# One layer of a Conformer, RWKV-7 and mixture-of-experts trunk: an earlier slot for small transposes, another order of loads, the last expert not split, the last store in two halves

## The chip, the cores and the metric

The kernel runs on one core of a Trainium2 chip. TensorE (PE) multiplies matrices; VectorE (DVE), ScalarE (ACT) and GpSimd (POOL) do the rest of the arithmetic, and SyncE (SP) issues most DMAs, in the order of its own program. Each engine runs its instructions in order and waits at semaphores. The metric is the time of one execution on the device, in microseconds (us), as the median of several runs; lower is better.

## The reference, cut to what matters

All data is float32. There are 520 tokens (512 of one prompt, 8 samples of one token each), a model width of 1024 and one layer.

```python
z = x @ w_in                                   # 2720 columns
u = z_a * sigmoid(z_gate)                      # group A: 512 channels
c = silu(layer_norm(causal_depthwise_conv(u, width=31)))
zs = z_rw + (z_prev - z_rw) * mu_shift         # group B: 8 heads of 64
r, k, v, wd, ad, gd = split(zs)
decay = exp(-exp(-softplus(-(w0 + tanh(wd) @ w_up)) - 0.5)); a = sigmoid(a0 + ad @ a_up)
S = S * decay + (S a_t) b_t^T + v_t k_t^T;  y_t = S r_t     # per token and head
x = layer_norm(ALPHA * x + concat(c, o_rw) @ w_out)
scores = sigmoid(x @ router_w)                 # 64 experts, 8 per token, group-limited
moe = shared_expert(x) + sum_e gate_e * ((silu(x @ G_e) * (x @ U_e)) @ D_e)
y = layer_norm(ALPHA * x + moe)
```

The kernel also returns the last conv inputs, the last shifted row and the recurrence state, for prompt and samples.

## The kernel before

The program has two blocks, with a meeting of all engines between them.

**Projection (`prepare`).** x is transposed, and the projection goes by columns of up to 128 outputs: `col(c)` does 8 steps over the contraction, with 2 matmuls of 260 tokens in each, so 16 matmuls; each shows as two records in the trace (float32). The order of the columns is `COLS`: two pairs for the conv gate (columns 0 to 3), the LoRA column (4), then k and r of each group of heads, and so on. `col(c, halfway)` calls `halfway()` after four of the eight steps, so that small work of PE sits inside a column. ACT drains a finished column out of PSUM (`drain`, L341 to L352), DVE shifts it (`shift`, L692 and L694) and, in between, adds up the 31 taps of the conv, one instruction per tap and channel group (`Taps.take`, L161 and L163; 124 in all). The number of taps between two steps is written out by hand.

Two helpers turn small inputs: `turn_small` transposes the conv weights, parameter vectors and shift rows, and waits for all 13 small loads (`small_loaded`), which ACT issues from 12.43 us on, after its copies of the transposed x; `turn_conv_rows` transposes the samples' conv rows (L492). DVE copies both out and does the samples' part of the conv (L659 to L679) before the first `glu` (L684) and the first taps. The loads of columns 4 and later each wait for the column four places before.

**Recurrence, mixing and routing (`recur_and_mix`).** The recurrence goes over 16 chunks of 32 tokens, with 16 steps on PE (L1392) and DVE (L1964 to L1997) in turn, and other work is put between the steps by tables (`CENTRE`, `TURN`, ...). SP's program is a list: waits and DMAs in one order. Of the names: `row_taken` counts PSUM tiles that ACT has drained, `step_done` the steps, `move_done` the chunk products; `w_out_half` are the two halves of w_out, used first by `mix_part` (L1498); `scr_y` is a detour through memory that lays the samples' y out as rows, read by `centre` (L1870) for the last but one tile; `load_up(sp, m, q)` and `load_down(sp, m, q)` fetch 1 MB each of expert q into slot q mod 6; `x_rows` are rows of x, needed for the layer norm after the mix.

**Experts (`experts`).** All 64 experts run in order, each on a list of up to 96 tokens. PE: `make_list` (L869), `gate_up` (L2297) for the next expert, `turn_list` (L2272) for the one after, `down` (L2325) for this one. ACT and DVE turn gate and up into the hidden values (`gate_act` L2306, `gate_mul` L2313 and L2315) and weigh the result (L2335 on ACT, L2343 on DVE). POOL adds the weighted rows to the tokens in memory with an indirect DMA (`add_rows`, L2352); each such scatter waits until the one before has landed:

```python
        pool.wait_ge(y_act, q + 1)
        pool.wait_ge(y_dve, q + 1)
        if job.has_before(1):
            pool.wait_ge(added[(s + 1) % 2], 16 * job.before)
```

For the last pair of experts the order is special: PE does the gate half of expert 63, then `down` of 62, then the up half of 63, then `down` of 63. After the last scatter SP reads the token rows back in five tiles, ACT and DVE normalise them (`shift_row`, L2261, is the last step of a tile), and SP stores them (L2388).

## Time and profile before

| | us |
|---|---|
| median of 3 runs | 1150.96 |
| all three runs | 1150.25, 1150.96, 1155.59 |
| profiled execution, time | 1150.96 |
| profiled execution, span from first to last instruction | 1148.6 |
| PE busy | 1081.4 |
| DVE busy | 537.3 |
| ACT busy | 280.1 |
| POOL busy | 180.3 |

The profile is of one execution. A row of the timeline gives start, duration, engine, line of the kernel, operation, the tensors written and read, shape, count, and in brackets how long the engine had been idle and who released it. PEld is PE's weight load, which runs beside its matmuls. PEclk is the clock that PE was granted: 1.00 is 2.4 GHz, 0.50 is 1.2 GHz. SPq and ACTq rows are DMA issues, not transfers.

### The profile page before, as it was taken

The page shows a single profiled execution, that of the slowest core. Times are in us where ns is not written, and L with a number is a line of the kernel's source. Part 1 is how long each engine was busy: PE and PEld are TensorE (multiplying, and loading weights), DVE is VectorE, ACT ScalarE, POOL GpSimd, SP SyncE. Part 2 cuts the span into 40 slices and gives each one's busy share as a digit, 9 for nine tenths or more (in the row PEclk, how much of TensorE's full clock was granted, in tenths as well). Part 3 has the DMA queues.
Part 4 walks back from the last instruction along what each step waited for, and adds up shares of the span by engine and source line. Part 5 has one row for each costly group of instructions (what it writes and reads, how often), then busy time and mean ns, then how long its engine had stood idle before and what let it go on. Part 6 is the DMA issues. An engine that isn't in the chain of part 4 may idle for free.

```text
span 1148.6 us, 33461 instructions
## 1 busy us (share of the span) xinstructions
PE 1081.4 (94%) x14966; PEld 820.4 (71%) x14967; DVE 537.3 (47%) x1204; ACT 280.1 (24%) x596; POOL 180.3 (16%) x198
## 2 busy tenths in 40 slices
PE   8999998888989999999999999999999999999990
PEld 6877886766653467777777777777777777777760
DVE  0888959699565787553222222222222222222215
ACT  2156411132427111111111111111111111111114
POOL 2000100000000002122222222222222122222310
PEclk9999998988679999999999999999999999999996
DMA  7222231320416547799999999999999999999724
GB/s 214 74 56 56 55 82 35 55 68 5 161 39 225 183 162 296 287 358 367 368 363 366 372 359 359 362 361 358 368 369 353 355 368 359 360 360 360 217 37 159
DMA packets 87364, 278.79 MB, mean 243 GB/s; under 512 B 22331, under 2 KB 46916, under 8 KB 62381
## 3 DMA queue, kind: packets, MB, share of 16 engines
q1 hardware_dynamic: 71941, 239.29, 56.9%
q0 software_dynamic: 14336, 34.11, 12.4%
q10 hardware_dynamic: 944, 3.24, 0.8%
q8 instruction: 119, 1.95, 0.7%
q14 instruction: 24, 0.20, 0.0%
HBM read 258.80 MB, written 34.52 MB: 255 GB/s over the span
## 4 chain that ended last, share of the span: by engine, by line
PE 67%; DVE 9%; ACT 2%; issue 2%; DMA 1%; SPq 0%; POOLq 0%; DVEq 0%; ACTq 0%
PE ph L2297 30%; PE ph L2325 19%; PE pst L2272 4%; PE ph L1498 2%; PE pz_late L2272 2%; DVE w_exp L163 2%; PE ph L1453 1%; PE pt L869 1%; PE pst L1392 1%; PE ph L1624 1%; PE ph L1480 1%; PE pz_late L1436 1%; PE pz_late L1437 1%; PE pt L1411 0%; PE pz_late L1521 0%
## 5 line engine op out<-in xcount | busy, mean ns | idle before, releaser
L2297 PE MATMUL ph<-arena,w_exp 128*64 128x96 f32 x8192 | 352.6, 247 | 0.0
L2297 PEld LDWEIGHTS ph<-arena,w_exp 128*64 128x64 f32 x8192 | 340.5, 138 | 4.2 <-issue 3.1
L2325 PE MATMUL ph<-w_exp,arena 128*96 128x512 f32 x512 | 230.5, 593 | 1.5 <-DVE arena L2315 1.5
L2352 POOL DMA_INDIRECT scr_f<-arena,row x64 | 91.9, 1436 | 472.2 <-DVE row L889 265.2
L2313 DVE TENSOR_TENSOR arena<-arena,ph 128x192 f32<-128x192 f32 x64 | 22.7, 354 | 294.3 <-ACT arena L2306 294.3
L507 PE MATMUL pz<-w_exp 128*128 128x260 f32 x672 | 158.8, 394 | 0.3 <-ACT w_exp L322 0.3
L2325 PEld LDWEIGHTS ph<-w_exp,arena 128*96 128x96 f32 x512 | 80.2, 167 | 104.0 <-issue 102.3
L507 PEld LDWEIGHTS pz<-w_exp 128*128 128x128 f32 x672 | 129.6, 196 | 23.7 <-issue 3.1
L2343 DVE TENSOR_SCALAR arena<-ph,weight 96x512 f32<-96x512 f32 x64 | 47.8, 746 | 168.0 <-PE ph L2325 167.9
L2306 ACT ACTIVATE arena<-ph 128x192 f32<-128x192 f32 x64 | 21.1, 330 | 426.1 <-PE ph L2297 419.4
L163 DVE SCALAR_TENSOR_TENSOR w_exp<-arena,w_exp 128x512 f32<-128x512 f32 x120 | 90.0, 750 | 3.8
L900 POOL DMA_INDIRECT x_area<-scr_x,row x64 | 63.4, 990 | 39.6 <-issue 34.1
L2335 ACT ACTIVATE arena<-ph,weight 96x512 f32<-96x512 f32 x64 | 43.7, 682 | 81.4 <-PE ph L2325 81.4
L1498 PE MATMUL ph<-w_exp 128*128 128x512 f32 x128 | 57.0, 597 | 1.2 <-DVE w_exp L2035 1.2
L2272 PE MATMUL pst<-ident,x_area 96*128 96x96 f32 x320 | 50.8, 289 | 0.0
L869 PEld LDWEIGHTS pt<-table,member 128*96 128x96 bf16 x320 | 24.3, 124 | 36.1 <-issue 35.7
L2272 PEld LDWEIGHTS pst<-ident,x_area 96*128 96x128 f32 x320 | 40.3, 202 | 7.7 <-issue 0.4
L1498 PEld LDWEIGHTS ph<-w_exp 128*128 128x128 f32 x128 | 23.6, 190 | 30.1 <-issue 28.4
L2282 ACT COPY arena<-pst 128x480 f32<-128x480 f32 x64 | 35.7, 558 | 35.0 <-PE pst L2272 33.9
L858 DVE TENSOR_TENSOR member<-slot_index,position 128x480 bf16<-128x480 f32 x64 | 41.6, 651 | 0.0
L2272 PE MATMUL pz_late<-ident,x_area 96*128 96x96 f32 x192 | 31.8, 275 | 0.0
L1480 PE MATMUL ph<-x_area,w_exp 128*128 128x260 f32 x128 | 29.1, 385 | 0.7 <-ACT arena L1829 0.7
(358 smaller groups left out, 1083.5 us busy)
## 6 DMA issues: line engine op xcount, KB each, us to landing
w_exp<-in_exp_up_dram SPq DMA_DIRECT2D x64, 1024.0 KB
w_exp<-in_exp_down_dram SPq DMA_DIRECT2D x64, 1024.0 KB
w_exp<-in_exp_gate_dram SPq DMA_DIRECT2D x64, 1024.0 KB
w_exp<-in_w_in_dram SPq DMA_DIRECT2D x22, 512.0 KB, 3.9
w_exp<-in_x_prompt_dram SPq DMA_DIRECT2D x8, 512.0 KB, 5.3
w_exp<-in_w_out_dram SPq DMA_DIRECT2D x2, 2048.0 KB, 11.5
scr_x<-arena SPq DMA_DIRECT2D x4, 512.0 KB
scr_f<-arena ACTq DMA_DIRECT2D x4, 512.0 KB, 4.5
```

The lines of the kernel that those rows point to most:

```text
L163: self.ch.link(self.nc.vector.scalar_tensor_tensor(out, u, w, out, ALU.mult, ALU.add))
L507: last = nc.tensor.matmul(banks(pz[0:w, c % 2, :])[:, b, :], m.w_col[:, c % WB, k, 0:w], halves(m.x_t[:, k, :])[:, b, :], start=(k == 0), ...
L858: nc.vector.tensor_tensor(m.member[:, s % 2], m.slot_index[:].unsqueeze(1).broadcast_to([P, NT, CAP]), src.unsqueeze(2).broadcast_to([P, N ...
L900: nc.gpsimd.indirect_dma_start(m.x_list[:, s, :], None, m.scr_x1, bass.IndirectOffsetOnAxis(ap=m.row[:, job.l:job.l + 1], axis=0), bounds_ ...
L1480: last = nc.tensor.matmul(banks(ph[:, 1 - part, :])[:, b, :], sh_w[part][:, k, j * P:(j + 1) * P], halves(x1_t[:, k, :])[:, b, :], start=( ...
L1498: last = nc.tensor.matmul(ph[0:n, i % 2, c * 512:(c + 1) * 512], lhs, w_out[c][:, kw, :], start=(part == 0 and k == 0), stop=(part == 1 an ...
L2272: last = nc.tensor.transpose(px[bank][:, at * CAP:(at + 1) * CAP], v[:, k, :], m.ident[0:CAP, 0:CAP])
L2297: last = nc.tensor.matmul(pgu[64 * half:64 * half + 64, s % 2, (2 * part + j) * CAP:(2 * part + j + 1) * CAP], w[job.slot][:, k, f0:P * ha ...
L2325: last = nc.tensor.matmul(pyl[0:CAP, c, :], hid[:, s % 2, j, :], m.expert_down[job.slot][:, j, c * 512:(c + 1) * 512], start=(j == 0), sto ...
L2335: nc.scalar.activation(y_list[:, s % 2, 0:512], pyl[0:CAP, 0, :], ACT.Copy, scale=weight[:, job.l:job.l + 1]).then_inc(y_act, 1)
L2343: nc.vector.tensor_scalar(y_list[:, s % 2, 512:1024], pyl[0:CAP, 1, :], weight[:, job.l:job.l + 1], None, ALU.mult).then_inc(y_dve, 1)
L2352: nc.gpsimd.indirect_dma_start(m.scr_f, bass.IndirectOffsetOnAxis(ap=row[:, job.l:job.l + 1], axis=0), y_list[:, s % 2, :], None, bounds_c ...
```

## The change

Four places change. First, `turn_small` moves from the middle of column 1 to behind column 0, and `turn_conv_rows` from the middle of column 2 to the middle of column 1. PE's instructions there, before (each row one kind of instruction with its count; `pz` is the projection's PSUM tile, `pt` the transposes'):

```order
L466 MATMUL pt<-ident,w_exp 128x128 x32
L469 MATMUL pt<-ident,w_exp 128x8 x8
L507 MATMUL pz<-w_exp 128x260 x24
L477 MATMUL pt<-ident,w_exp 128x39 x4
L482 MATMUL pt<-ident,w_exp 128x9 x14
L482 MATMUL pt<-ident,w_exp 32x9
L507 MATMUL pz<-w_exp 128x260 x16
L492 MATMUL pt<-ident,w_exp 128x120 x8
L507 MATMUL pz<-w_exp 128x260 x56
```

and in the changed kernel:

```order
L466 MATMUL pt<-ident,w_exp 128x128 x32
L469 MATMUL pt<-ident,w_exp 128x8 x8
L507 MATMUL pz<-w_exp 128x260 x16
L477 MATMUL pt<-ident,w_exp 128x39 x4
L482 MATMUL pt<-ident,w_exp 128x9 x14
L482 MATMUL pt<-ident,w_exp 32x9
L507 MATMUL pz<-w_exp 128x260 x8
L492 MATMUL pt<-ident,w_exp 128x120 x8
L507 MATMUL pz<-w_exp 128x260 x72
```

Sixteen matmuls are column 0, 24 are one and a half columns. The transposes of L477 and L482 are `turn_small`, those of L492 `turn_conv_rows`; eight matmuls moved from ahead of the first to behind it, and sixteen from ahead of the second to behind.

Second, SP's list in the second block has the loads of w_out ahead of the samples' detour through `scr_y`, drops the wait for the last step ahead of the x rows, and has two expert loads ahead of the waits for the layer-norm rows. Before:

```order
L1193 DMA scr_y<-arena 128x32
L1195 DMA x_area<-scr_y 8x512
L1198 DMA w_exp<-in_w_out_dram 128x8x512 x2
L1200 DMA arena<-in_router_w_dram 128x8x64
L1201 DMA arena<-in_router_bias_dram 128x64
L1205 DMA w_exp<-in_x_prompt_dram 128x1024 x2
L1208 DMA w_exp<-in_ln_g_dram 128x1024
L1209 DMA w_exp<-in_ln_b_dram 128x1024
L1210 DMA w_exp<-in_sh_up_dram 128x8x256
L1211 DMA w_exp<-in_sh_down_dram 128x2x1024
L919 DMA w_exp<-in_exp_up_dram 128x2048
L925 DMA w_exp<-in_exp_down_dram 128x2048 x2
```

and changed:

```order
L1195 DMA w_exp<-in_w_out_dram 128x8x512 x2
L1197 DMA scr_y<-arena 128x32
L1199 DMA x_area<-scr_y 8x512
L1201 DMA arena<-in_router_w_dram 128x8x64
L1202 DMA arena<-in_router_bias_dram 128x64
L1205 DMA w_exp<-in_x_prompt_dram 128x1024 x2
L920 DMA w_exp<-in_exp_up_dram 128x2048
L926 DMA w_exp<-in_exp_down_dram 128x2048
L1210 DMA w_exp<-in_ln_g_dram 128x1024
L1211 DMA w_exp<-in_ln_b_dram 128x1024
L1212 DMA w_exp<-in_sh_up_dram 128x8x256
L1213 DMA w_exp<-in_sh_down_dram 128x2x1024
```

The two `w_out` loads moved up by two rows, and expert 1's up and expert 0's down from the end of this piece to behind the x rows (expert 3's down follows it).

Third, the last pair of experts has the common order. The end of PE's expert work (L2297 is gate and up, 64 matmuls; L2325 is down, 4), before:

```order
L2297 MATMUL ph<-arena,w_exp 64x96 x64
L2272 MATMUL pst<-ident,x_area 128x96 x5
L2272 MATMUL pz_late<-ident,x_area 128x96 x3
L2325 MATMUL ph<-w_exp,arena 96x512 x4
L2297 MATMUL ph<-arena,w_exp 64x96 x32
L2325 MATMUL ph<-w_exp,arena 96x512 x4
L2297 MATMUL ph<-arena,w_exp 64x96 x32
L2325 MATMUL ph<-w_exp,arena 96x512 x4
```

and changed:

```order
L2298 MATMUL ph<-arena,w_exp 64x96 x64
L2274 MATMUL pst<-ident,x_area 128x96 x5
L2274 MATMUL pz_late<-ident,x_area 128x96 x3
L2325 MATMUL ph<-w_exp,arena 96x512 x4
L2298 MATMUL ph<-arena,w_exp 64x96 x64
L2325 MATMUL ph<-w_exp,arena 96x512 x8
```

The second half (up) of expert 63 moved ahead of `down` of 62. ACT and DVE follow: `gate_act` and `gate_mul` of 63 stand ahead of the weighing of 62.

Fourth, the last tile's last DVE step and its store are split into two halves of 512 columns.

```diff
@@ projection, PE
                 col(0)
-                col(1, turn_small)
-                col(2, turn_conv_rows)
+                turn_small()
+                col(1, turn_conv_rows)
+                col(2)
@@ second block, SP
+                sp.wait_ge(row_taken, use["col", 2 * LATE - 1] + 1)
+                for c in range(2):
+                    sp.dma_start(m.w_out_half[c][:], ...).then_inc(m.w_out_loaded[c], 16)
                 sp.wait_ge(sample_y_ready, 1)
                 sp.dma_start(m.scr_y..., s_y[:]).then_inc(sample_y_stored, 16)
                 sp.wait_ge(sample_y_stored, 16)
                 sp.dma_start(sample_y, m.scr_y).then_inc(sample_y_loaded, 16)
-                sp.wait_ge(row_taken, use["col", 2 * LATE - 1] + 1)
-                for c in range(2):
-                    sp.dma_start(m.w_out_half[c][:], ...).then_inc(m.w_out_loaded[c], 16)
...
                 sp.wait_ge(move_done, 2 * TM)
-                sp.wait_ge(step_done, NCH)
                 for i in range(2):
                     sp.dma_start(x_rows[:, i, :], ...).then_inc(x_loaded[i], 16)
+                load_up(sp, m, 1)
+                load_down(sp, m, 0)
                 sp.wait_ge(y_done, TM)
                 sp.wait_ge(state_ready, NCH + 1)
...
-                load_up(sp, m, 1)
-                load_down(sp, m, 0)
                 load_down(sp, m, 3)
@@ shift_row(dve, at, i, parts=1)
+        for c in range(parts):
+            cs = slice(D // parts * c, D // parts * (c + 1))
+            nc.vector.scalar_tensor_tensor(f_scaled[i][0:n, cs], ...).then_inc(out_ready, 1)
@@ experts, SP: the last store
+        for c in range(2):
+            sp.wait_ge(out_ready, NT + c)
+            cs = slice(D // 2 * c, D // 2 * (c + 1))
+            sp.dma_start(m.y_prompt[T - P:T, cs], f_scaled[TM - 1][:, cs]).then_inc(out_stored, 16)
@@ experts, PE
-                gate_up(pe, Job(q + 1), (0, 1) if q + 2 < E else (0,))
+                gate_up(pe, Job(q + 1))
...
             down(pe, Job(q))
-            if q + 2 == E:
-                gate_up(pe, Job(q + 1), (1,))
@@ experts, DVE (ACT alike)
-            if q + 2 < E:
+            if q + 1 < E:
                 gate_mul(dve, Job(q + 1))
...
             weigh_dve(dve, Job(q))
-            if q + 2 == E:
-                gate_mul(dve, Job(q + 1))
@@ the last tile
-        shift_row(dve, TM, TM - 1)
+        shift_row(dve, TM, TM - 1, 2)
```

## Rows read from the trace of the kernel before

**Rows 1.** Page, part 1: engine, busy us (share of the span), instructions.
```profile
PE 1081.4 (94%) x14966; PEld 820.4 (71%) x14967; DVE 537.3 (47%) x1204; ACT 280.1 (24%) x596; POOL 180.3 (16%) x198
```

**Rows 2.** Windows: stretch, length, busy us by engine, PEclk, DMA share, GB/s.
```profile
300.00:360.00 60.00, 53.02 (x783) 32.09 (x772) 34.20 (x60) 28.67 (x79) 0.00 (x0) 0.80 0.54 182
560.00:700.00 140.00, 140.00 (x2084) 108.77 (x2083) 36.53 (x126) 25.70 (x55) 33.78 (x28) 1.00 1.02 365
```

**Rows 3.** Timeline, PE at the start: start us, us, what, [idle before <-releaser].
```profile
12.69 10.79 PE L507 MATMUL pz<-w_exp 128*128 128x260 f32 x48 [0.30 <-ACT w_exp L322]
23.65 0.44 PE L477 MATMUL pt<-ident,w_exp 39*128 39x39 f32 x4 [0.18 <-DMA w_exp<-in_state_conv_dram]
25.00 7.28 PE L507 MATMUL pz<-w_exp 128*128 128x260 f32 x32
```

**Rows 4.** Timeline, all engines, the same columns, 32 to 70 us.
```profile
32.73 1.22 DVE L665 COPY w_exp<-pt 128x480 f32<-128x480 f32 x2 [7.20 <-PE pt L492]
37.90 0.70 DVE L684 TENSOR_TENSOR arena<-arena 128x520 f32<-128x520 f32 x1
51.28 0.71 ACT L352 ACTIVATE w_exp<-pz,w_exp 128x520 f32<-128x520 f32 x1
56.48 0.75 DVE L692 SCALAR_TENSOR_TENSOR w_exp<-arena,w_exp 128x512 f32<-128x512 f32 x1
58.13 1.11 PE L514 MATMUL pa<-w_exp,arena 64*128 64x260 f32 x4 [0.47 <-ACT w_exp L413]
69.11 0.75 DVE L692 SCALAR_TENSOR_TENSOR w_exp<-arena,w_exp 128x512 f32<-128x512 f32 x1 [2.99 <-ACT w_exp L352]
```

**Rows 5.** Windows of 1 us, PE alone: length, busy, PEclk, DMA.
```profile
257.00:258.00 1.00, 0.00 (x0) 1.00 0.00 0
258.00:259.00 1.00, 0.00 (x0) 1.00 0.00 0
260.00:261.00 1.00, 1.00 (x14) 0.50 0.07 16
263.00:264.00 1.00, 1.00 (x5) 0.92 0.00 0
```

**Rows 6.** Timeline of SP; then page, part 6: issues, KB, us to landing.
```profile
297.41 0.35 SPq L1193 DMA_DIRECT2D scr_y<-arena  x1
300.94 1.03 SPq L1198 DMA_DIRECT2D w_exp<-in_w_out_dram  x2
w_exp<-in_w_out_dram SPq DMA_DIRECT2D x2, 2048.0 KB, 11.5
```

**Rows 7.** Chain of waits in order of time: start us, us, what.
```profile
327.70 0.57 DVE arena L1870
343.63 3.63 PE ph L1498 x8
```

**Rows 8.** Timeline, all engines, the last expert.
```profile
1113.91 2.86 PE L2297 MATMUL ph<-arena,w_exp 128*64 128x96 f32 x64
1115.61 1.40 POOL L2352 DMA_INDIRECT scr_f<-arena,row  x1 [4.99 <-DVE arena L2343]
1118.22 3.67 PE L2325 MATMUL ph<-w_exp,arena 128*96 128x512 f32 x8 [1.45 <-DVE arena L2315]
1121.94 0.75 DVE L2343 TENSOR_SCALAR arena<-ph,weight 96x512 f32<-96x512 f32 x1 [3.77 <-PE ph L2325]
1123.53 1.40 POOL L2352 DMA_INDIRECT scr_f<-arena,row  x1 [6.52 <-DVE arena L2343]
```

**Rows 9.** Chain of waits, the last scatter.
```profile
1123.53 4.73 DMA scr_f<-arena,row
```

**Rows 10.** The scatter tensor scr_f: DMA time from issue to landing.
```profile
DMA to landing us min/median/max: 3.7/8.6/10.3
```

**Rows 11.** Timeline, the last row of the output.
```profile
1144.30 1.28 DVE L2261 SCALAR_TENSOR_TENSOR w_exp<-w_exp,arena 128x1024 f32<-128x1024 f32 x1
```

**Rows 12.** Windows of 1 us, DVE alone, DMA share and GB/s last.
```profile
1145.00:1146.00 1.00, 0.58 (x1) 0.50 0.97 389
```

More of the change, by code:

```diff
@@ L1191, in _ @@
                         sp.dma_start(m.new_shift_s[:, c0:c0 + w], tail_rows[1:1 + B, t % 2, 0:w]).then_inc(tails_stored[t % 2], 16)
+                sp.wait_ge(row_taken, use["col", 2 * LATE - 1] + 1)
+                for c in range(2):
+                    sp.dma_start(m.w_out_half[c][:], m.w_out[:, c * 512:(c + 1) * 512].rearrange("(k p) n -> p k n", p=P)).then_inc(m.w_out_loaded[c], 16)
                 sp.wait_ge(sample_y_ready, 1)
@@ L1195, in _ @@
                 sp.dma_start(sample_y, m.scr_y).then_inc(sample_y_loaded, 16)
-                sp.wait_ge(row_taken, use["col", 2 * LATE - 1] + 1)
-                for c in range(2):
-                    sp.dma_start(m.w_out_half[c][:], m.w_out[:, c * 512:(c + 1) * 512].rearrange("(k p) n -> p k n", p=P)).then_inc(m.w_out_loaded[c], 16)
                 sp.wait_ge(w2_done, TM)
@@ L2255, in invert_root, with shift_row @@
         nc.vector.reciprocal(aggr[0:n, i, 3:4], aggr[0:n, i, 2:3]).then_inc(inverted, 1)
-    def shift_row(dve, at, i):
+    def shift_row(dve, at, i, parts=1):
         n = TOK_TILES[i][1]
@@ L2260, in shift_row @@
         dve.wait_ge(scaled, at + 1)
-        nc.vector.scalar_tensor_tensor(f_scaled[i][0:n, :], f_scaled[i][0:n, :], aggr[0:n, i, 3:4], ln2_b[0:n, :],
-                                       ALU.mult, ALU.add).then_inc(out_ready, 1)
+        for c in range(parts):
+            cs = slice(D // parts * c, D // parts * (c + 1))
+            nc.vector.scalar_tensor_tensor(f_scaled[i][0:n, cs], f_scaled[i][0:n, cs], aggr[0:n, i, 3:4], ln2_b[0:n, cs],
+                                           ALU.mult, ALU.add).then_inc(out_ready, 1)
     def turn_list(pe, job):
@@ L2283, in copy_turned, with gate_up @@
                            px[bank][:, 0:(k1 - k0) * CAP].rearrange("p (k t) -> p k t", t=CAP)).then_inc(x_ready, 1)
-    def gate_up(pe, job, parts=(0, 1)):
+    def gate_up(pe, job):
         q, s = job.q, job.s
@@ L2289, in gate_up @@
             pe.wait_ge(hid_ready, q - 1)
-        for part in parts:
-            w = (m.expert_gate, m.expert_up)[part]
+        for part, w in enumerate((m.expert_gate, m.expert_up)):
             pe.wait_ge((m.gate_loaded, m.up_loaded)[part][job.slot], job.filled)
@@ L2299, in gate_up @@
                                                 start=(k == 0), stop=(k == KD - 1))
-        if 1 in parts:
-            last.then_inc(gu_done, 1)
+        last.then_inc(gu_done, 1)
     def gate_act(act, job):
@@ L2383, in sync @@
             sp.dma_start(f[i][0:n, :], m.scr_f[t0:t0 + n, :]).then_inc(f_loaded[i], 16)
-        for at, i in enumerate(ORDER):
+        for at, i in enumerate(ORDER[:-1]):
             t0, n = TOK_TILES[i]
@@ L2388, in sync @@
             sp.dma_start(dst, f_scaled[i][0:n, :]).then_inc(out_stored, 16)
-        sp.wait_ge(out_stored, 16 * NT)
+        for c in range(2):
+            sp.wait_ge(out_ready, NT + c)
+            cs = slice(D // 2 * c, D // 2 * (c + 1))
+            sp.dma_start(m.y_prompt[T - P:T, cs], f_scaled[TM - 1][:, cs]).then_inc(out_stored, 16)
+        sp.wait_ge(out_stored, 16 * (NT + 1))
     def tensor(pe):
@@ L2527, in scalar @@
         for q in range(E):
+            if q + 1 < E:
+                gate_act(act, Job(q + 1))
             if q + 2 < E:
-                gate_act(act, Job(q + 1))
                 copy_turned(act, Job(q + 2))
             weigh_act(act, Job(q))
-            if q + 2 == E:
-                gate_act(act, Job(q + 1))
         def body(k, ex):
```

## The prediction

> **What bounds the kernel now.** I read the page first. PE is busy for 94% of the span [rows 1]: 67 us of idle time is all that any reordering can touch, unless it takes work away, and this change takes none. Next came the windows by stage. From 560 to 700 us PE is busy for 140.00 of 140 us at full clock [rows 2]; the 64 experts run like that from about 480 to 1100 us, one after the other, with PE never waiting for a weight, though the DMA engines are as full as PE. Nothing in the change touches that stretch, so it only slides in time. What is left are four places where instructions move: the first columns of the projection, SP's queue around the recurrence, the last expert, and the last store. For these I read PE's timeline at both ends, VectorE's (DVE) and ScalarE's (ACT) beside it, SP's issues, and the chain of waits.
>
> In the projection PE and DVE take turns at being last. PE starts its columns at 12.69 us and runs them without a gap of note [rows 3]. DVE sits idle for 7.20 us until the transposes at L492 are there, starts its tap work at 37.90, and then leads for a while: at 58.13 PE waits 0.47 us for a tanh (L413) whose input DVE shifts at 56.48. At 69.11 it has turned round: DVE waits 2.99 us for the drain of column 6, which comes straight behind PE's matmuls [rows 4].
>
> **The small transposes.** Before, they stand in the middle of column 1 and find their data just landed: PE waits 0.18 us at 23.65 for the last of the small loads [rows 3]. The order now puts them behind column 0. Issue of those loads is not changed (ACT issues them after its copies of x), so they still land at 23.6. The work taken from in front of them is half a column: 16 of the 32 records that take 7.28 us [rows 3], 3.64 us. So PE reaches them at about 20.0 and stands for about 3.65 us. Nothing is gained back on PE: the half column is still to be done. Column 1 ends 4.5 us later (its second half, and L492 too, now follow), column 2 and all after it 3.64 later.
>
> DVE gains at first. L492 has 16 matmuls less ahead of it and, with the stall, comes 3.5 us earlier, so its small work and the first taps start that much sooner. It would reach the shift of the LoRA column (L692, 56.48) at 53.0. But the drain of that column ended at 51.28+0.71=51.99 [rows 4] and comes 3.64 later, at 55.6. DVE goes on at 55.6, 0.9 us sooner than before, which takes away PE's 0.47 us at 58.13; PE is then 3.64-0.47=3.17 us late. At 69.11 DVE was already waiting for PE's column, so it is 3.17 late too, and DVE, PE and ACT go through the rest of the projection with the same distances. All engines meet at the end of this part, near 224 us. I take 3.2 us, whole, on the path. Bounds from the rows: 0 if later waits of this kind swallow it, 3.7 if the 0.47 is not won back.
>
> **The clock behind that stall.** The slices from 257 to 259 us hold no work of PE; its granted clock, 1.00 (2.4 GHz) in them, is 0.50 (1.2 GHz) at 260, with PE working again, and 0.92 at 263 [rows 5]. Such a stretch of some 3.3 us at half clock costs 1.7 us when the work in it is dense. The new stall is longer than those two slices, so I expect a fall behind it. Ends: 0 (the clock holds) and 1.7. I take 1.3, as part of the stretch may lie in the stall itself. The Trainium skill (TensorE: Matmul & The Clock Gate, section "HAM oscillation — how this bites in real kernels") says that a wait for a DMA between dense groups of matmuls can bring the clock down each time; by that rule the case with the fall stands, 1155.6 us, and without it the sum would be 1154.3. The rows agree with the rule at 256 us.
>
> **SP's queue.** The load of w_out, 4 MB, goes from 300.94 to where the store of scr_y stood, 297.41 [rows 6]. Its first user is the mix at 343.63 [rows 7], over 40 us later: nothing gained. Behind it now queue on SP the store and reload of the sample rows; they may land as late as w_out does, 11.5 us after its issue [rows 6], with about 3 us more for the way out and back (300.94 less 297.41 is 3.5): about 312 us. Their reader is the centring of the last but one tile (L1870) at 327.70 [rows 7], so 15 us of cover remain, and with both sides shifted by the same 3 to 5 us it stays so. The x rows no longer wait for step 16, and loads of expert 1's up and expert 0's down go ahead of the layer-norm rows; these 3 MB run between 312 and 325 us, when nothing else loads. Behind the wait that remains, the layer-norm rows meet 2 MB less in front of the shared weights. No PE or DVE wait in the profile ends on any of these, so I price it at 0. Bounds: 0.5 us either way, about the 0.47 that a wait cost in [rows 4]; the covers named would have to vanish for more.
>
> **The last expert.** Before: gate of 63, down of 62, up of 63, a wait of 1.45 us for the ACT/DVE steps, down of 63. Now gate and up of 63, down of 62 (under which those steps hide), down of 63. PE ends 1.45 us sooner. But down of 62 ends 2.86 us later (the up part, [rows 8]). POOL's scatter of 62 started at 1115.61 and would start at 1118.5. Each scatter waits for the one before to land; the last took 4.73 us from POOL's start [rows 9]. So 62 lands at 1123.2. The last scatter started at 1123.53, 0.84 us after its DVE step (1121.94+0.75=1122.69). Now its DVE step is ready at 1121.2, but the landing at 1123.2 holds it; with 0.1 to 0.84 us to get going it starts between 1123.3 and 1124.1. I take 1123.7: 0.2 us later than before, so PE's gain is gone. Bounds: -1.45 (all of it comes through) and +0.6. With the shortest landing of the run, 3.7 us [rows 10], it would be -0.9.
>
> **The last store.** The last DVE step took 1.28 us for 1024 columns [rows 11]; 512 cost 0.75 (L692, [rows 4]), so both halves end 0.2 us later, the first 0.5 us sooner. The store of the tile before is still running at 1145 to 1146, 389 GB/s with the engines at 0.97 [rows 12]: the halves queue behind it, and their 512 KB take 1.35 us as before. Only the small gap between two stores can close. I take -0.1; bounds -0.5 and +0.3. The Trainium skill (DMA: Bandwidth & Descriptors, section "Anatomy of one DMA — SWDGE (gpsimd) path") gives a DMA a fixed 2.0 us plus bytes over 436 GB/s; by that an estimate for the half as last store would be 0.6 us less, minus the 0.2 on DVE. That fit is for another kind of queue, and no run here shows it.
>
> **Sum.** 3.2 + 1.3 + 0 + 0.2 - 0.1 = 4.6 us. The profiled execution has a span of 1148.6 us and a time of 1150.96 us, which is also the median of the three runs. 1150.96+4.6 = 1155.6 us, 0.4% slower.
>
> **Rivals.**
> The clock holds (0.14): only the stall remains, 1154.3 us. For it: the stall follows full-clock work, and the wait of 1.45 us at the last expert leaves the clock at 1.00. Against: [rows 5].
> The early start of DVE decides (0.08), the other side: if DVE's tap work and not PE's columns sets the end of the projection, the 3.5 us that DVE gains at 32.73 come through, and with +0.1 at the end the time is 1147.5 us. It decides if the 2.99 us wait at 69.11 goes away. Against: that wait is DVE's, for PE [rows 4]. About a third of this case, with luck elsewhere, would read as faster by over 0.5%.
> The last expert pays (0.08): the scatter of 62 lands fast enough that the 1.45 us come through: 1154.0 us.
> More half clock in the recurrence (0.20): between 300 and 360 us the granted clock is 0.80 on average [rows 2], which is 24 us at half clock, in stretches behind short idle times of PE. All of that is shifted against whatever decides when the clock is looked at. The three runs before lie 5.3 us apart; a further 2 to 3 stretches at 1.7 us each are 4.4 us: 1160 us.
>
> **How the numbers follow.** The main case has 0.50, its own range is 1153.5 to 1158. A measurement of this kernel can tell about 0.5% (5.8 us) from no change, so over 1156.7 us counts as slower. Of the main case I give 0.14 to that side and 0.36 to the same. Slower: 0.14+0.20=0.34. Same: 0.36+0.14+0.05+0.08=0.63. Faster: 0.03. The range runs from 1151.5 to 1160: below it lies most of the DVE case, above it half of the clock case.
>
> **What would show it.** A PE idle of 3.5 to 3.8 us in front of L477 at 23.6, on a DMA; a clock of 0.50 in some slice between 23 and 29; the drains of columns 2 to 5 some 3.6 us later; DVE's small work from 29.3; the LoRA shift waiting for ACT at 55.6; the next part starting 3 to 5 us later. At the end: no wait before the last L2325, and the last scatter waiting for a scatter, not for DVE. It would be wrong if the small loads landed at 20, if the projection ended no later than before, or if the experts, from first to last, took another time than before.

## The result: about 9 us slower, and outside the range

The changed kernel took 1162.8 us (median of 5 runs, 1160.7 to 1163.3) against 1153.0 us for the kernel before beside it: a ratio of 1.0077, 95% interval 1.0049 to 1.0104. Run once more beside its parts (e8 below) it was 1.0082 [1.0066, 1.0099], 9.5 us. The prediction said 1155.6 us, 1151.5 at least and 1160 at most. The base also moved: the kernel before, 1150.96 us in the three runs shown, had medians of 1153.0 to 1155.1 in the comparisons, and its profile is of a quick execution. So ratios are compared here, not times. On the base that the prediction used, the two ratios are 1159.8 and 1160.4 us, the edge of its range; the change itself is twice the 4.6 us that it forecast.

| stretch | before | changed | more |
|---|---|---|---|
| start to block 2 (DVE's first row of it) | 224.1 | 230.7 | 6.6 |
| block 2 to the issue of ln_g | 119.6 | 124.9 | 5.3 |
| from there to the gate of expert 63 | 763.8 | 764.6 | 0.8 |
| gate of 63 to the end of the span | 41.1 | 42.2 | 1.1 |
| span | 1148.6 | 1162.4 | 13.8 |

The profiled pair is further apart than the medians, 13.8 us against 9 to 10, because that execution of before was quick in its first stretch. The page's first part of the changed kernel answers to [rows 1]; PE's busy time is nearly the same, so the loss is idle time:

```profile
PE 1083.0 (93%) x14966; PEld 821.7 (71%) x14967; DVE 537.4 (46%) x1205; ACT 280.8 (24%) x596; POOL 179.9 (15%) x198
```

The windows of the changed kernel, as in [rows 2] (length, busy time by engine, PEclk, DMA share, GB/s). The experts run as before. From 300 to 360 us PE works 5.3 us less (all is shifted, so it is not the same work), at a lower clock:

```profile
300.00:360.00 60.00, 47.75 (x1037) 33.31 (x1032) 32.24 (x59) 21.36 (x60) 0.83 (x4) 0.77 0.43 145
560.00:700.00 140.00, 140.00 (x2059) 107.88 (x2060) 37.13 (x126) 26.00 (x56) 32.15 (x27) 1.00 1.03 359
```

The same work compared, block 2 up to the issue of ln_g (PE alone: length, busy, PEclk, DMA share, GB/s), the kernel before first: PE is busy 0.9 us less and its mean clock is no lower, but it is idle for 22.8 us and not 16.6. So what this stretch lost is idle time, not clock:

```profile
224.09:343.69 119.60, 103.02 (x2944) 0.81 0.22 69
230.66:355.60 124.94, 102.12 (x2944) 0.82 0.25 83
```

PE's timeline at the start, changed kernel, as in [rows 3] (start us, us, what, idle before and releaser):

```profile
12.13 7.28 PE L507 MATMUL pz<-w_exp 128*128 128x260 f32 x32 [0.30 <-ACT w_exp L322]
24.38 0.65 PE L477 MATMUL pt<-ident,w_exp 39*128 39x39 f32 x4 [4.96 <-DMA w_exp<-in_state_conv_dram]
24.96 1.68 PE L482 MATMUL pt<-ident,w_exp 9*128 9x9 f32 x15
26.57 6.57 PE L507 MATMUL pz<-w_exp 128*128 128x260 f32 x16
```

The wait is there, 4.96 us and not 3.65: the columns begin 0.56 us sooner than in [rows 3], and the transposes, which wait for the last load, 0.73 us later. Behind it 16 records of the projection take 6.57 us; in [rows 3] 32 take 7.28, so 16 are 3.64. The clock had already fallen inside the wait, and stayed down. Windows of 1 us show both ends of the stretch:

```profile
23.00:24.00 1.00, 0.00 (x0) 0.00 (x0) 0.00 (x0) 0.00 (x0) 0.00 (x0) 0.50 0.55 167
31.00:32.00 1.00, 1.00 (x4) 0.74 (x3) 0.00 (x0) 0.00 (x0) 0.00 (x0) 0.50 0.00 0
33.00:34.00 1.00, 1.00 (x10) 1.00 (x9) 0.41 (x1) 0.00 (x0) 0.00 (x0) 1.00 0.00 0
```

DVE, as in [rows 4]. The copy of L492 begins at 33.59, 0.86 us later than before, not 3.5 earlier; the slow half column took the gain. The waits for ACT's drains are 2.66 us at the LoRA shift and 4.59 at the shift of column 6, r (2.99 before):

```profile
33.59 1.22 DVE L666 COPY w_exp<-pt 128x480 f32<-128x480 f32 x2 [6.50 <-PE pt L492]
59.97 0.75 DVE L693 SCALAR_TENSOR_TENSOR w_exp<-arena,w_exp 128x512 f32<-128x512 f32 x1 [2.66 <-ACT w_exp L352]
76.48 0.75 DVE L693 SCALAR_TENSOR_TENSOR w_exp<-arena,w_exp 128x512 f32<-128x512 f32 x1 [4.59 <-ACT w_exp L352]
```

SP's timeline, as in [rows 6]: w_out goes at 304.45, the detour's store behind it, and its reload only at 319.18, 13.7 us after the store (3.2 before):

```profile
304.45 1.03 SPq L1195 DMA_DIRECT2D w_exp<-in_w_out_dram  x2
305.52 3.71 SPq L1197 DMA_DIRECT2D scr_y<-arena  x1
319.18 0.30 SPq L1199 DMA_DIRECT2D x_area<-scr_y  x1
```

No engine waits for those sample rows: DVE reads them at 342.82 (L1870). But PE stands, a few us behind the issue of w_out, in the middle of its chunk products (L1376) and of a step (L1392), for "issue", that is for nothing that the profile shows. First the kernel before, then the changed one:

```profile
300.85 0.27 PE L1376 MATMUL ph<-w_exp 32*64 32x64 f32 x2 [0.62 <-issue]
304.84 1.00 PE L1392 MATMUL pst<-x_area,w_exp 64*64 64x64 f32 x13 [1.41 <-issue]
```
```profile
311.70 0.27 PE L1376 MATMUL ph<-w_exp 32*64 32x64 f32 x2 [3.63 <-issue]
318.07 1.01 PE L1392 MATMUL pst<-x_area,w_exp 64*64 64x64 f32 x13 [2.40 <-issue]
```

The same instructions of the program, with 2.03 us of idle time before and 6.03 now. The page's part 3 has a queue for instructions, with the same row in both kernels (packets, MB, share), and one window of 0.5 us, from 309.0, in the changed kernel has one packet of it inside PE's idle time, with the DMA engines full of w_out (third fence, a window of 2 us: DMA share 1.06, 392 GB/s last):

```profile
q8 instruction: 119, 1.95, 0.7%
```
```profile
q8 instruction: 1, 0.02, 13.5%
```
```profile
308.00:310.00 2.00, 0.07 (x3) 0.00 (x0) 1.93 (x5) 1.09 (x5) 0.00 (x0) 1.00 1.06 392
```

119 packets for 1.95 MB are 16 KB each. PE and its weight load have 29,933 instructions in the span, some 250 for each packet, and the packets come as PE's instructions do: 3.3 to 4.2 us apart among the small matmuls of the recurrence, 6 to 10 us apart in the experts. So it looks as if blocks of PE's instructions were fetched while the program runs, by the same DMA engines that move w_out. That became the theory to test. (The Trainium skill, Trainium Architecture — The Big Picture, section "The software stack", says that the instruction streams are moved into the engines' memories when the program is loaded. By the row above that is not all: 119 packets of an instruction queue lie inside the span.)

The last expert, changed kernel, as in [rows 8, 9] (PE, POOL, DVE):

```profile
1120.23 5.50 PE L2298 MATMUL ph<-arena,w_exp 128*64 128x96 f32 x128
1125.67 7.11 PE L2325 MATMUL ph<-w_exp,arena 128*96 128x512 f32 x16
1130.97 1.40 POOL L2352 DMA_INDIRECT scr_f<-arena,row  x1 [7.63 <-DVE arena L2343]
1132.81 0.75 DVE L2343 TENSOR_SCALAR arena<-ph,weight 96x512 f32<-96x512 f32 x1 [2.69 <-PE ph L2325]
1136.38 1.40 POOL L2352 DMA_INDIRECT scr_f<-arena,row  x1 [4.00 <-DMA scr_f<-arena,row]
```

PE has no gap any more; the last scatter waits for the scatter before, not for DVE. From the start of gate of 63 to the last scatter it is 16.15 us, against 1123.53 - 1107.51 = 16.02 before.

The last store, as in [rows 11, 12]. The two halves end at 1158.58, 22.20 us after the last scatter's start (22.05 before), and the span ends 3.82 us later (3.02 before); a little data still moves at 1161:

```profile
1157.16 1.42 DVE L2263 SCALAR_TENSOR_TENSOR w_exp<-w_exp,arena 128x512 f32<-128x512 f32 x2
1157.94 0.99 SPq L2392 DMA_DIRECT2D out_dram<-w_exp  x2
```
```profile
1160.00:1160.50 0.50, 0.00 (x0) 0.00 (x0) 0.00 (x0) 0.00 (x0) 0.00 (x0) 0.50 1.02 381
1161.00:1161.50 0.50, 0.00 (x0) 0.00 (x0) 0.00 (x0) 0.00 (x0) 0.00 (x0) 0.50 0.06 8
```

### The profile page after: what moved, and what is told of

Read it like the earlier page. It is cut to its first block, busy times and chain, and to the rows that moved or that the text cites. A ratio compares the mean times of both kernels' runs of the same rounds, so it can differ in the third digit from the quotient of the medians.

```text
span 1162.4 us, 33461 instructions
## 1 busy us (share of the span) xinstructions
PE 1083.0 (93%) x14966; PEld 821.7 (71%) x14967; DVE 537.4 (46%) x1205; ACT 280.8 (24%) x596; POOL 179.9 (15%) x198
## 3 DMA queue, kind: packets, MB, share of 16 engines
q8 instruction: 119, 1.95, 0.7%
## 4 chain that ended last, share of the span: by engine, by line
PE 65%; DVE 9%; issue 2%; DMA 2%; ACT 2%; DVEq 0%; POOLq 0%; SPq 0%; ACTq 0%
PE ph L2298 30%; PE ph L2325 19%; PE pst L2274 4%; PE ph L1498 2%; PE pz_late L2274 2%; DVE w_exp L163 2%; PE pt L870 1%; PE ph L1453 1%; PE pst L1392 1%; DMA scr_f<-arena,row 1%; PE ph L1480 1%; PE pz_late L1436 1%; DMA x_area<-scr_x,row 1%; PE pz_late L1437 1%; PE pz_late L1521 0%
## 5 line engine op out<-in xcount | busy, mean ns | idle before, releaser
L2325 PE MATMUL ph<-w_exp,arena 128*96 128x512 f32 x512 | 230.2, 592 | 0.0
L507 PE MATMUL pz<-w_exp 128*128 128x260 f32 x672 | 161.5, 399 | 0.3 <-ACT w_exp L322 0.3
L2325 PEld LDWEIGHTS ph<-w_exp,arena 128*96 128x96 f32 x512 | 80.3, 167 | 102.9 <-issue 102.8
L859 DVE TENSOR_TENSOR member<-slot_index,position 128x480 bf16<-128x480 f32 x64 | 41.5, 651 | 0.0
## 6 DMA issues: line engine op xcount, KB each, us to landing
w_exp<-in_exp_up_dram SPq DMA_DIRECT2D x64, 1024.0 KB, 16.8
```

The source lines that it names most:

```text
L507: last = nc.tensor.matmul(banks(pz[0:w, c % 2, :])[:, b, :], m.w_col[:, c % WB, k, 0:w], halves(m.x_t[:, k, :])[:, b, :], start=(k == 0), ...
L859: nc.vector.tensor_tensor(m.member[:, s % 2], m.slot_index[:].unsqueeze(1).broadcast_to([P, NT, CAP]), src.unsqueeze(2).broadcast_to([P, N ...
L2325: last = nc.tensor.matmul(pyl[0:CAP, c, :], hid[:, s % 2, j, :], m.expert_down[job.slot][:, j, c * 512:(c + 1) * 512], start=(j == 0), sto ...
```

## The experiments

All are timed against the kernel before, beside it on the same chip. The us are the ratio's, times 1154. "P" is the start of block 2, "R" the time from there to the issue of ln_g, "idle" PE's two gaps with no releaser at L1376 and L1392, all from the one profile of each kernel (a dash where no such gap is listed; a line number can be off by up to 2 in a variant). One profile is one execution, and P and R differ by 3 to 4 us between kernels with the same instructions there.

| | ratio [95%] | us | P | R | idle |
|---|---|---|---|---|---|
| before | | | 224.1 | 119.6 | 0.6, 1.4 |
| whole change | 1.0077 [1.0049, 1.0104] | +8.9 | 230.7 | 124.9 | 3.6, 2.4 |
| e1 slot | 1.0029 [1.0013, 1.0044] | +3.3 | 227.9 | 119.5 | 0.6, 0.9 |
| e2 w_out early | 1.0014 [0.9999, 1.0029] | +1.6 | 225.2 | 125.1 | 2.0, 2.4 |
| e3 other loads | 0.9997 [0.9972, 1.0022] | -0.3 | 225.8 | 119.5 | 0.6, 1.1 |
| e4 tail | 1.0014 [0.9999, 1.0030] | +1.6 | 224.2 | 116.7 | 0.3, 0.9 |
| e5 early small loads | 1.0027 [1.0013, 1.0042] | +3.1 | 225.1 | 123.2 | 0.3, 3.1 |
| e6 slot, early small loads | 1.0014 [1.0000, 1.0028] | +1.6 | 227.7 | 123.2 | 0.3, 3.6 |
| e7 w_out late | 0.9995 [0.9983, 1.0008] | -0.6 | 226.3 | 119.8 | 0.3, 1.1 |
| e8 whole change again | 1.0082 [1.0066, 1.0099] | +9.5 | 230.5 | 124.6 | 1.7, 3.8 |
| e9 slot, w_out early | 1.0061 [1.0041, 1.0081] | +7.0 | 227.7 | 126.8 | 3.4, 2.1 |
| e10 split wait | 0.9978 [0.9959, 0.9998] | -2.5 | 223.6 | 123.5 | 0.7, 3.6 |
| e11 slot, split wait | 1.0038 [1.0020, 1.0057] | +4.4 | 228.9 | 123.3 | 0.7, 3.6 |
| e12 change without slot | 1.0041 [1.0025, 1.0057] | +4.7 | 225.5 | 123.3 | 0.3, 4.7 |
| e13 split wait, w_out late | 0.9963 [0.9941, 0.9984] | -4.3 | 221.5 | 120.7 | 0.7, 1.4 |
| e14 change, w_out late | 1.0038 [1.0022, 1.0055] | +4.4 | 230.6 | 121.1 | -, 1.5 |
| e15 half of w_out early | 1.0003 [0.9985, 1.0020] | +0.3 | 222.8 | 120.7 | 1.7, 0.2 |
| e16 detour late | 0.9985 [0.9968, 1.0001] | -1.7 | 226.5 | 118.3 | 0.3, 1.1 |

**e1 to e4: the four parts alone.** e1:

```diff
                 col(0)
-                col(1, turn_small)
-                col(2, turn_conv_rows)
+                turn_small()
+                col(1, turn_conv_rows)
+                col(2)
```

> The kernel before with the earlier slot for the small transposes alone. Theory 1 (stall plus slow clock behind it): PE stands 4.5 to 5 us in front of L477, the transposes and the first half of column 1 run at half clock (some 3 us more), and block 2 starts 6 to 7 us later than before (224.09); time +6 to +7.5 us. Theory 2 (the sum as predicted, the rest of the loss lies in SP's queue): block 2 starts 3 to 4.6 us later, time +4.5. Theory 3 (shifting the recurrence is what costs, whatever shifts it): block 2 starts 6.5 us later and the recurrence takes 4 to 5 us longer as well, time +11 or more.

Measured +3.3 us, block 2 3.8 us later than in the profile before. PE waits 4.59 us in front of L477, with half clock from 22 to 30 us. That is the wait and the clock of theory 1, but the size of theory 2: the slot costs about what was predicted for it. The recurrence is no longer for it (R 119.5), which ends theory 3.

e2, the loads of w_out ahead of the detour (the first hunk of SP's list in the diff above, alone):

> The kernel before with the loads of w_out ahead of the samples' detour alone. Theory 1 (PE stands beside this load for want of instructions, 3.6 us in L1376): the projection is as before, PE shows an idle stretch of 2 to 4 us with no releaser in L1371 to L1381 within 10 us of the issue of w_out, and the time is +2 to +5 us. Theory 2 (as predicted): no such idle time, sample rows land by 315 us, time 0 +-0.5 us. Theory 3 (the 3.6 us belong to the shift of everything by the projection): no idle time here, the time within 1 us of before.

Measured +1.6 us, at the edge of what can be told. The profile has theory 1's mark: the gap in L1376 is 1.99 us and the one in L1392 2.40, and R is 5.5 us longer. The time, +1.6, is under the 2 to 5 us that theory 1 named. Theory 2 gave no idle time, theory 3 none without the shift; both fall.

e3, the wait for step 16 away and the two expert loads earlier, alone:

> The kernel before with the x rows no longer behind step 16 and with expert 1's up and expert 0's down ahead of the layer-norm rows, alone. Theory 1 and 2 both: 0 +-1 us, no new idle time of PE. If transfers beside the recurrence starve PE in general, one more PE idle stretch with no releaser, beside these 3 MB, and +1 to +3 us.

Nothing, as expected: -0.3 us, with an interval of some 3 us either way.

e4, the last expert not split and the last store in two halves:

> The kernel before with the last expert not split and the last store in two halves, and nothing else. As predicted: +0.2 for the last expert (start of gate of 63 to start of the last scatter 16.1 us against 15.95 before) and -0.1 for the store: +0.1 us in all. As read in the changed kernel's trace: +0.1 and, for the store, +0.8 (3.8 us from the end of the last DVE step to the end of the span against 3.0), +0.9 us. Both lie inside what the times can tell, so the trace decides: the stretch from the start of gate of 63 to the end.

From gate of 63 to the end the trace has 42.2 us (1104.58 to 1146.8), against 41.1, 40.9, 40.9 and 41.0 in before, e1, e2 and e3, and 42.2 in the whole change. The last DVE step ends 3.8 us before the end, 3.0 to 3.1 in those four. So the tail costs 1.1 to 1.3 us, most of it behind the last DVE step; as read, not as predicted. Over all profiles it is 42.1 to 42.4 us in the five with the changed tail and 40.9 to 41.5 in the thirteen without.

**e5 and e6: the slot with its data there.** ACT's issues of the small rows move ahead of its copies of x:

```diff
+                act.dma_start(par_rows[0:CW, :], m.conv_w).then_inc(small_loaded, 16)
+                ...   (the vectors of PARAMS, state_shift, mu_shift)
                 for g in range(XT_GROUPS):
                     act.wait_ge(xt_turned, g + 1)
```

> The kernel before, in its own order, with the small parameter and shift rows fetched ahead of ACT's copies of x instead of behind them (the state_conv rows stay behind). In three of the four profiles that have the order of before up to L477, PE waits 1.05 to 1.42 us there for the small loads, landing 11.8 to 12.2 us after the start of the columns. Theory 1: the loads land by 20, the wait goes, -1 us (0 to -2), if the start of the columns at 12.1 does not slip. Rival: DVE and not PE decides there and the time is that of before.

> The earlier slot for the small transposes together with the earlier small loads, so that the slot has its data. Theory 1 (all that the earlier slot costs is PE's wait for the loads and the clock behind it): no wait over 1 us in front of L477, no half clock behind it, and the time equals that of the earlier loads alone, 1 us under before. Rival, the early start of DVE pays: DVE's small work and first taps begin some 3.5 us sooner than before, block 2 starts sooner than with the earlier loads alone, time 2 to 4 us under before. Rival, the order itself costs: 3 us over before even without the wait.

The condition failed: the start of the columns slipped, from 12.0 to 12.7 us in the old order to 16.4 and 16.8, because x arrived later (in e5 PE waits 7.8 us for it instead of 4.6). So neither is faster than before, and the gain expected for e5 did not come. What they still show is the difference between them, with neither a wait in front of L477 nor half clock behind it. In time the two are the same within their intervals (medians 1155.5 with the slot, 1156.8 without). Block 2 starts 2.6 us later with the slot in the two profiles, but 2.0 of these were lost ahead of the moved transposes, in column 0, whose 32 records take 7.28 us in all other kernels with the slot. In e6, PE's timeline:

```profile
16.82 9.32 PE L507 MATMUL pz<-w_exp 128*128 128x260 f32 x32 [0.30 <-ACT w_exp L327]
```

So neither an early start of DVE that pays 2 to 4 us nor an order that costs 3 us by itself is borne out.

**e7: w_out late.**

```diff
-                sp.wait_ge(row_taken, use["col", 2 * LATE - 1] + 1)
-                for c in range(2):
-                    sp.dma_start(m.w_out_half[c][:], ...)
...
                 sp.wait_ge(move_done, 2 * TM)
+                for c in range(2):
+                    sp.dma_start(m.w_out_half[c][:], ...)
```

> The kernel before with the 4 MB of w_out issued behind the last chunk product instead of ahead of the router loads, some 13 us later. Theory 1 (PE's instructions come late beside this transfer): the idle times of PE with no releaser at L1376 and L1392, 0.6 and 1.4 us in the profile before, 2.0 and 2.4 with w_out earlier, become 0.6 and 0.9 or less; block 2 from its start to the issue of ln_g takes 1 to 2 us less than 119.5; time -1 to -2 us. Theory 2 (these idle times and the length of block 2 have to do with the sample rows' detour, not with w_out): unchanged, 0.

The idle times are 0.3 and 1.1 us, about as theory 1 said, but R is that of before (119.8), and the time too: -0.6 us, not -1 to -2. At its old place w_out can miss the fetches: in the profiles of before, e1, e3 and e4 it is issued 76 to 77 us into block 2, and an instruction packet goes at 77 to 78, just behind the issue. The next one comes over 6 us later, and in before it finds PE at matmuls of about 1 us each (L1436 and L1437), with no idle time.

**e8: the change again.**

> The whole change again, beside the same runs of before as its parts. The four parts alone came to ratios of 1.0029, 1.0014, 0.9997 and 1.0014, 6.2 us in sum, with their intervals some 4 us wide; the whole had 1.0077. If the parts add, the ratio is 1.004 to 1.007. If they work on one another (a later start of the recurrence together with the earlier w_out), it is 1.008 or more again, and block 2 takes 5 us longer than 119.6.

Again 9.5 us, with as much half clock as in the changed kernel's first profile. The four parts came to 6.2 us in sum; each is known to some 1.5 to 3 us only, so this alone does not show that they work on one another.

**e9 and e12: the slot with w_out, and all but the slot.** e9 is e1 and e2 together:

> The earlier slot for the small transposes and the earlier w_out together, nothing else of the change. Alone they came to +3.3 and +1.6 us, the whole change to +9.4, of which the tail's trace explains 1.2. Theory 1 (the parts add): +5 us, ratio 1.004. Theory 2 (the two work on one another): +8 us, ratio 1.007, with some 70 us of half clock up to 360 us, as in the whole change, against 61 us before.

> The whole change with the small transposes back in their old places: the loads of w_out and the others, the last expert and the last store as changed. If the parts add: +1.6 - 0.3 + 1.6 = +2.9 us (ratio 1.0025). If the slot is what tips the recurrence into more half clock, the rest costs no more than that. If the earlier w_out does it with the earlier expert loads behind it, +6 us (1.005).

e9 had +7.0 us, nearer to theory 2's 8 than to 5. Its gaps are 3.4 and 2.1 us, R is 126.8, and half clock up to 360 us comes to 68 us (61 before, 72 in the change), the more of it behind the slot at 22 to 30 us. e12 had +4.7 where the parts sum to 2.9. Both put the earlier w_out at 3 to 4 us and not at 1.6. But the intervals are 3 to 5 us wide: whether it costs more beside the other parts than alone is not shown, and e2 may only have come out low. The slot costs 9.5 - 4.7 = 4.8 us inside the whole change and 3.3 alone, the same within the intervals too.

**e10 and e11: two waits for the small loads.**

```diff
-                    pe.wait_ge(small_loaded, 16 * (1 + len(PARAMS) + 4))
+                    pe.wait_ge(small_loaded, 16 * (1 + len(PARAMS) + 2))
...
+                    pe.wait_ge(conv_rows_loaded, 32)     # in turn_conv_rows
```

> The kernel before with two waits for the small loads: the transposes at L477 wait for the 11 small rows only, those of the conv rows (L492 of before) for the two loads of state_conv, which are issued and land last. Theory 1 (PE's wait of about 1.2 us and the stretch of half clock behind it, 25 to 31 us, cost something): no wait in front of the transposes, no half clock there, -1 to -2.5 us. Rival (DVE or later work takes it back): 0.

> The earlier slot with the same two waits. If the 11 small rows land by about 20 us, PE's wait of 4.6 us there shrinks to under 1.5 us. Theory 1 (the slot costs by that wait and the clock behind it alone): time 0 to -2 us against before, the same as the two waits without the slot within 1 us. Rival, the order costs by itself (with earlier loads block 2 started 2.5 us later in this order than in the old one): +2 us or more over the two waits without the slot. Rival, the early start of DVE pays: 2 us or more under it.

e10 is faster than before, -2.5 us, as theory 1 said: PE's wait is 0.23 us, and there is no half clock between 24 and 110 us. e7's profile shows what it replaces in the old order, PE's timeline:

```profile
24.57 0.44 PE L477 MATMUL pt<-ident,w_exp 39*128 39x39 f32 x4 [1.17 <-DMA w_exp<-in_state_conv_dram]
...
25.93 8.97 PE L507 MATMUL pz<-w_exp 128*128 128x260 f32 x32
```

A wait of 1.17 us, and the 32 records behind it take 8.97 us where [rows 3] has 7.28. Of the eight profiles with the old order and the old small loads six wait 1.0 to 1.4 us here and one 2.4, and in four of these seven half clock follows; only the profile that the prediction was made from has 0.18. e11 missed its condition: PE, released by the last of the 11 small rows (mu_shift), starts the transposes at 23.4 only, not at 20. So the slot still waits 3.5 us, with half clock from 23 to 31. It costs 6.9 us over e10 (some 3 us either way), and block 2 starts 5.3 us later: the slot's price against an order that pays neither wait nor clock.

**e13 to e16: what w_out does.**

> The kernel before with the two waits for the small loads and w_out issued behind the last chunk product. Theory 1 (fetches of PE's instructions that fall into w_out's transfer come late; the wait for state_conv brings the clock down): no idle time of PE without a releaser over 1.4 us in the recurrence, block 2 119.8 us or less, time -2.5 to -4 us. Theory 2 (the clock alone decides, w_out's place is nothing): -2.5 us as with the two waits alone, block 2 as often 123.5 as 119.6.

> The whole change, but w_out issued behind the last chunk product. Theory 1: PE's idle times at L1376 and L1392 are 0.3 to 1.3 us as with w_out late before, block 2 takes 120 us instead of 124.9, and the time is +4.5 to +5.5 us over before instead of +9.4. Theory 2 (the slot's shift of the recurrence is what makes it longer): block 2 123 us or more, +7.5 or more.

> w_out's first half (2 MB) issued early, as in the change, its second half behind the last chunk product. Its transfer then ends some 6 us after its issue, between two fetches of PE's instructions (at 77 and 83 us from the start of block 2 with w_out early). Theory 1: PE's idle time at L1376 stays long (2.0 to 3.6 us as in the change), the one at L1392 falls to 1.4 or less (2.1 to 4.7 in the change); block 2 takes 120 to 123 us. Rival (the samples' detour decides): it lands 6 us sooner, and both idle times change alike. Rival (clock alone): no relation to the transfer.

> The kernel before with the samples' detour (scr_y out and back) and then w_out behind the last chunk product. The sample rows then come back some 92 us after the start of block 2, as late as in the change, but nothing large is transferred beside the dense part of the recurrence. Theory 1: as with w_out late alone, idle times up to 1.3 us, block 2 119.8 us, time within 1 us of before. Rival (the late sample rows are what the earlier w_out costs): block 2 123 us or more and +1.5 to +4 us.

e14 had +4.4 us instead of 9.5, R is 121.1: moving this one load takes 5 us off the change (some 2.5 either way), as theory 1 said. e15 is the sharpest. PE's timeline:

```profile
300.47 0.37 PE L1376 MATMUL ph<-w_exp 32*64 32x64 f32 x2 [1.71 <-issue]
304.96 1.00 PE L1392 MATMUL pst<-x_area,w_exp 64*64 64x64 f32 x13 [0.17 <-issue]
```

With 2 MB instead of 4 the first gap stays (1.71 us, a little under the 2.0 named) and the second is gone (0.17; 2.1 to 4.7 us in the five profiles with all of w_out early). e16 brings the sample rows back as late as in the change and is no slower, so the detour is not the cause. e10's profile shows the same with w_out at its old place: there the detour came back sooner, w_out went 75.7 us into block 2, a packet of instructions followed at 81.8 in the middle of the transfer, and PE stood 3.60 us (e5, e6 and e11 alike, 3.1 to 3.6 us):

```profile
307.92 1.01 PE L1394 MATMUL pst<-x_area,w_exp 64*64 64x64 f32 x14 [3.60 <-issue]
```

The packets' times tie the gaps to the fetches more closely still. The 18 profiles have 67 gaps of PE of over 1 us with no releaser between 40 and 110 us of block 2, and in every one PE resumes 2.1 to 3.1 us after an instruction packet began; with packets at least 3.3 us apart as a rule, chance would put about a quarter of them there. With w_out's transfer across them, the packets of the 14 longest gaps at L1376 and L1392 (1.7 to 4.7 us) began 4.9 to 7.0 us after the packet before; in the four kernels with w_out late the packets up to these gaps are 3.3 to 4.4 us apart.

Over all profiles R goes with this: 118.3 to 121.1 us in the five with w_out late or half of it early; 116.7 to 119.6 in four with it at its old place and the second gap under 1.5 us, 123.2 to 123.5 in four where that gap is over 3; 123.3 to 126.8 in the five with it early.

e13, the two waits together with w_out late, is the fastest kernel of the case: 1151.1 us against 1155.1 beside it, 0.9963 [0.9941, 0.9984]. That is within the interval of e10, so theory 2's -2.5 us is not ruled out by the time; its R, 120.7 against 123.5, and its gaps are those of theory 1.

## Why the prediction was wrong, step by step

- **The stall of PE and the clock behind it** (3.2 + 1.3 = 4.5 us) was right as a sum: +3.3 us alone, +4.7 inside the change, and block 2 starts at 229.5 us on average in the five profiles with the slot against 225.0 in eight without it, 4.5 later. Its parts were off: the wait is 4.6 to 5.0 us and not 3.65, and the half clock lasts 7 to 10 us and covers half a column and the transposes, not 3.3 us. The wait of [rows 5], from which the clock's cost was taken, was one of 3.07 us for DVE, not for a DMA, and the fall behind it was shorter. Nor are the 67 us of idle time all that a reordering can touch: half clock shows as busy time, and these 7 to 10 us of it were new. Against that, the old order pays a wait in most executions and half clock in some, which the quick profile of before didn't show.
- **DVE's gain of 3.5 us** never came: the half column ahead of L492 ran at half clock. The rival built on it fell with e6.
- **SP's queue, priced at 0 ± 0.5**, is the step that failed. The covers named there hold: no engine waits for the sample rows or for w_out. (In the kernel before, the row of L1870 that reads the sample rows is the one at 330.47, not at 327.70. The x rows and expert loads ran from 326 us on, not from 312, as a wait for the chunk products still stands ahead of them; e3 shows no cost.) What was left out is who else uses the DMA engines from 304 to 316 us: by all that the runs show, PE's own instructions, and PE stands while they come. The earlier load costs 1.6 us alone, 3.7 beside the slot (7.0 less 3.3), 5.1 in the whole change (9.5 less 4.4 in e14, where it stands late, not at its old place). R says 125.0 on average with it early and 121.1 at its old place, 3.9 us.
- **More half clock in the recurrence** was a rival at 0.20, with a time of 1160 us. Its sign and size were near, by luck: there was no more of it. The mean clock of block 2 is 0.81 before and 0.82 changed, some 45 us at half clock in both. e1 shifts everything and has R 119.5.
- **The last expert**, +0.2: measured +0.1 (16.15 us to the last scatter against 16.02), by the mechanism given (the scatter of 62 holds the last one).
- **The last store**, -0.1 with +0.3 as its upper bound: measured +0.9, of which 0.1 is DVE's second instruction and 0.8 lies behind it. The data of the halves did not close up with the store before; what the trickle at 1161 waits for was not tried apart.
- Summed by the traces: 4.5 + 3.9 + 1.1 = 9.5 us, which is what e8 measured; averages of profiles that differ by some 3 us among themselves, so the last tenths agree by luck. The absolute time was also missed by 2 us through the base.

The Trainium skill (TensorE: Matmul & The Clock Gate, section "HAM oscillation — how this bites in real kernels") says that a wait for a DMA between groups of matmuls brings the clock down and that the next group then starts slow. The trace agrees: PEclk is 0.50 inside the wait of 4.96 us and for some 8 us behind it. But there is also a fall behind a wait of only 1.17 us (e7), and none behind one of 2.40 us at the same place (e16: PEclk 1.00 from 22 to 34 us). The length of the wait alone does not decide here.

What stays open: why e16 keeps its clock; why the half clock behind the slot lasts until 33 us in the three profiles of the whole change (with or without its w_out) and until 30 or 31 in e1, e9 and e11, which have the same order of work up to there. And that the fetch is what PE waits for is inferred from the packets' times, from the two gaps that come and go with the transfer (e2, e7, e14, e15), and from e16; no profile names it as a releaser. Why a packet comes late beside the transfer was not tried apart.

## What to carry to other kernels

An engine that runs through small instructions quickly can be held up by its instruction fetches, and here these used the DMA engines: look at idle time put down to "issue" beside the stretches in which the DMA engines are full, and place multi-megabyte loads where the engine runs few, long instructions, even if that makes them later; "nobody waits for this load" doesn't price moving it. Where PE is made to wait between dense matmuls, price the work behind the wait at half clock as well, and check in more than one execution whether the wait of before is typical.

## What the runs showed of the hardware

- Instruction packets of 16 KB, 119 in the span, on the DMA engines, one for some 250 instructions of PE and its weight load; among the small matmuls of the recurrence one goes every 3.3 to 4.2 us. Where one fell into a transfer at 380 to 400 GB/s, PE stood 1.7 to 4.7 us at L1376 or L1392. With no large transfer beside it PE also stood, but shorter: 0.2 to 1.5 us at these two places, up to 1.9 some 50 us into block 2.
- Small row loads issued ahead of everything delayed x, which is 2 MB: the columns started at 16.4 us (e5) and not at 12.0 to 12.7, for 11 small loads.
- A store of 512 KB in two halves ended 0.8 us later behind the last DVE step than one store: 3.8 to 3.9 us in the change, e4, e8, e12 and e14, 3.0 to 3.1 in the thirteen other profiles.
- Behind a wait of 4.6 to 5.0 us of PE for a DMA the clock was at half for 7 to 10 us, part of it inside the wait; behind waits of 1.0 to 2.4 us at the same place it fell in four profiles of seven, and the one with 2.4 kept it.
